# Nine blocks of each layer's down projection as seven block products instead of eight, with sums on VectorE

## What is computed

```
D_MODEL, SEQ, DEPTH, D_FF = 2048, 256, 2, 5632
def conv_ffn(x, w_gate, w_up, conv_w, conv_b, w_down):
    g, u = x @ w_gate, x @ w_up
    gc = conv_b + causal 3-tap convolution of g
    return (silu(gc) * u) @ w_down        # (256 x 5632) @ (5632 x 2048)
for l in range(DEPTH):
    x = layer_norm(ALPHA * x + mixer(x), ln1_g[l], ln1_b[l])
    x = layer_norm(ALPHA * x + conv_ffn(x, ...), ln2_g[l], ln2_b[l])
```

## Time and profile before

| what | value |
|---|---|
| median of 3 runs | 2224.84 us (2224.28 to 2224.9) |
| span of the profiled execution (its own time isn't given beside it) | 2222.5 us |
| PE busy | 2208.0 us, 99% |
| DVE, ACT, POOL busy | 1397.8, 1037.8, 244.1 us |
| first down stage, from the start of the span | 868.3 to 1107.8 us |
| second down stage | 1973.8 to 2213.5 us |

### The profile page before, as it was taken

One profiled execution on the slowest core, in us unless ns is written; L12 is line 12 of the kernel. 1 busy time (PEld: TensorE's weight loads), 2 busy tenths in 40 slices (PEclk: granted clock), 3 DMA queues, 4 the chain that ended last, 5 costly groups with the idle time before them and its releaser, 6 DMA issues.

```text
span 2222.5 us, 28282 instructions
## 1 busy us (share of the span) xinstructions
PE 2208.0 (99%) x11424; PEld 1892.6 (85%) x11424; DVE 1397.8 (63%) x1758; ACT 1037.8 (47%) x1295; POOL 244.1 (11%) x250
## 2 busy tenths in 40 slices
PE   9999999999999999999999999999999999999998
PEld 7888888888888888888888888888888888888886
DVE  6655576776667666544485566677766666664545
ACT  5444555444444444433454445554444444443343
POOL 1751000220000000000008410002200000000000
PEclk9999999999999999999999999999999999999999
DMA  8655565666666666666665555756666666666664
GB/s 278 194 167 160 157 215 174 189 190 190 190 190 189 190 189 205 219 192 193 190 190 170 162 162 150 225 173 189 189 190 189 190 189 190 189 211 215 191 195 155
DMA packets 214818, 420.92 MB, mean 189 GB/s; under 512 B 13056, under 2 KB 15136, under 8 KB 213664
## 3 DMA queue, kind: packets, MB, share of 16 engines
q1 hardware_dynamic: 211824, 406.37, 59.8%
q0 software_dynamic: 2432, 12.22, 1.6%
q10 hardware_dynamic: 432, 0.52, 0.1%
HBM read 416.97 MB, written 2.10 MB: 189 GB/s over the span
## 4 chain that ended last, share of the span: by engine, by line
PE 98%; DVE 1%; DMA 0%; ACT 0%; issue 0%; POOLq 0%; POOL 0%; SPq 0%; DVEq 0%
PE ps L1289 29%; PE ps L1177 16%; PE ps L1175 16%; PE ps L1176 16%; PE ps L1293 15%; PE ps L1220 1%; PE ps L1416 1%; PE ps L1390 1%; PE ps L1367 1%; DMA raw<-in_w_in_dram 0%; PE ps L1423 0%; PE ps L1163 0%; PE ps L1436 0%; PE ps L1437 0%; PE ps L1435 0%; PE ps L1454 0%
## 5 line engine op out<-in xcount | busy, mean ns | idle before, releaser
L820 DVE TENSOR_TENSOR wlo<-raw,whi 128x1024 fp32r<-128x1024 f32 x767 | 964.7, 1264 | 700.6 <-ACT whi L578 697.0
L578 ACT ACTIVATE whi<-raw 128x1024 fp32r<-128x1024 f32 x767 | 807.9, 1059 | 853.0 <-DMA raw<-in_w_down_dram 278.5
L1289 PE MATMUL ps<-xT,whi 128*128 128x512 f32 x2816 | 657.3, 390 | 0.0
L1289 PEld LDWEIGHTS ps<-xT,whi 128*128 128x128 f32 x2816 | 522.6, 188 | 104.3 <-ACT qkT L599 0.4
L1175 PE MATMUL ps<-whi,xT 128*128 128x512 f32 x920 | 369.0, 401 | 0.0
L1177 PE MATMUL ps<-whi,xT 128*128 128x512 f32 x920 | 359.3, 391 | 0.0
L1176 PE MATMUL ps<-wlo,xT 128*128 128x512 f32 x920 | 358.5, 390 | 0.0
L1293 PEld LDWEIGHTS ps<-xT,wlo 128*128 128x128 f32 x2816 | 350.6, 192 | 7.5
L1293 PE MATMUL ps<-xT,wlo 128*128 128x256 f32 x2816 | 352.9, 283 | 0.0
L1175 PE MATMUL ps<-whi,hT 128*128 128x512 f32 x696 | 270.9, 389 | 0.0
L1177 PE MATMUL ps<-whi,hT 128*128 128x512 f32 x696 | 270.9, 389 | 0.0
(11 more groups left out here) (203 smaller groups left out, 1203.5 us busy)
## 6 DMA issues: line engine op xcount, KB each, us to landing
raw<-in_w_gate_dram SPq DMA_DIRECT2D x176, 512.0 KB, 4.0
raw<-in_w_up_dram SPq DMA_DIRECT2D x176, 512.0 KB, 4.0
raw<-in_w_down_dram SPq DMA_DIRECT2D x176, 512.0 KB, 4.1
raw<-in_w_in_dram SPq DMA_DIRECT2D x175, 512.0 KB, 3.7
raw<-in_w_out_dram SPq DMA_DIRECT2D x64, 512.0 KB, 4.2
xres<-in_x_dram POOLq DMA_DIRECT2D x4, 512.0 KB, 5.7
lnb<-in_ln_g_dram POOLq DMA_DIRECT2D x2, 1024.0 KB, 7.5
lnb<-in_ln_b_dram POOLq DMA_DIRECT2D x2, 1024.0 KB, 10.4
```

Of the source, the lines that this page charges most:

```text
L578: act.activation(whi[:, s, :, :], raw[:, s, :, :], ACT.Copy).then_inc(hi_done, 1)
L820: dve.tensor_tensor(wlo[:, s, :, :], raw[:, s, :, :], whi[:, s, :, :].bitcast(F32), ALU.subtract)\
L1289: return pe.matmul(ps[:, bank, :], whi[:, s, kk, m * P:(m + 1) * P], xT[:, kt, :, :].rearrange("p a s -> p (a s)"), start=kt == 0, stop=kt ...
```

## The change

Take a pair of hidden tiles and two neighbouring chunks of columns (a half). The eight block products (2 token tiles x 2 hidden tiles x 2 chunks) become seven products of sums of blocks, by Strassen's method in Winograd's form. This is done for 5 pairs in half 0 (chunks 0, 1) and 4 pairs in half 1 (chunks 2, 3): nine **sets** a layer, numbered 0 to 8. Each takes the place of two groups; 70 groups stay, and group numbers below are the new ones. PE does set k right behind group `SET_AFTER[k]`.

```diff
+SETS_AT = ((11, 16, 20, 24, 28), (36, 41, 46, 51))
+SETS = [(half, i) for half in range(2) for i in range(len(SETS_AT[half]))]
+SET_AFTER = [SETS_AT[half][i] for half, i in SETS]
+SET_LOAD = [-1] + SET_AFTER[:-1]
+HALF_GROUPS = [2 * (GD - len(a)) for a in SETS_AT]
+PRODUCTS = ("A12", "S4", "A11", "S1", "S3", "S2", "A22")
+FACTORS = ("B21", "B22", "B11", "T1", "T3", "T2", "T4")
+TARGET = (0, 2, 4, 5, 7, 6, 1)
+SUMS = (((4,), (4, 6, 5)), ((4, 6, 7), (4, 6, 7, 5)))
...
+        sraw = nc.alloc_sbuf_tensor_at("sraw", [P, 7, CW], F32, offset=xT_at)
+        slo = nc.alloc_sbuf_tensor_at("slo", [P, 7, CW], F32R, offset=xT_at)
+        shi = nc.alloc_sbuf_tensor_at("shi", [P, 7, CW], F32R, offset=xT_at + 7 * CW * 4)
...
 SP
+                for n in range(DOWN):
+                    c, _, pair = down_group(n)
+                    load(w_down, layer, 0, BASE_DOWN + n, pair * GK, c * CW)
+                    if n - RING in SET_LOAD:
+                        k = SET_LOAD.index(n - RING)
...
+                        if layer + k > 0:
+                            sp.wait_ge(set_used, set_count(layer, k - 1))
+                        for kk in (1, 0):
...
+                            sp.dma_start(sraw[:, 2 * kk:2 * kk + 2, :].rearrange("p s n -> p (s n)"),
+                                         w_down[layer, row:row + P, half * 2 * CW:(half + 1) * 2 * CW])\
+                                .then_inc(set_in, 16)
...
 POOL
+                pool.wait_ge(set_used, set_count(layer, len(SETS) - 1))
                 carry_wait(pool, 3)
                 pool.dma_start(lnb2[:, 0, :], row(ln2_g, layer).broadcast_to([P, D_MODEL])).then_inc(ln2_in, 16)
-                wait_groups(pool, layer, BASE_DOWN + GD // 2)
                 pool.dma_start(lnb2[:, 1, :], row(ln2_b, layer).broadcast_to([P, D_MODEL])).then_inc(ln2_in, 16)
...
 ACT, behind split_hi of group n
+                for k, a in enumerate(SET_LOAD):
+                    if k < PREPARED and n == max(a + 6, 8):
+                        form_high(layer, k)
+                    part = n - max(a + 6, 8)
+                    if 0 <= part < 3:
+                        set_high(layer, k, part)
...
 DVE, behind split_lo of group n
+                for k, a in enumerate(SET_LOAD):
+                    at = max(a + 6, 8)
+                    if k < PREPARED and n == at - 1:
+                        form_sums(layer, k)
+                    if k < PREPARED and n == at + 1:
+                        form_low(layer, k)
+                    if n == at:
+                        set_sum(layer, k)
+                    if 0 < n - at < 4:
+                        set_low(layer, k, n - at - 1)
+                for half in range(2):
+                    summed = SETS_AT[half][-2] + 9
+                    if n == summed:
+                        y_chunk(layer, 1, 2 * half, in_banks(2 * half))
+                    if n == summed + 1:
+                        products(layer, 2 * half)
+                    if n == summed + 2:
+                        products(layer, 2 * half + 1)
+                if n == DOWN_ENDS[1] + LAG:
+                    y_chunk(layer, 1, 1, in_banks(1))
...
 PE
+            def set_of_products(layer, k):
...
+                for i, (name, factor) in enumerate(zip(PRODUCTS, FACTORS)):
+                    bank, first, last = TARGET[i], pair == 0, pair == len(SETS_AT[half]) - 1
+                    if first and bank == 2:
+                        wait_free(pe, layer, 2, ("down", 2 * half + 1))
+                    if first and bank >= 4:
+                        wait_free(pe, layer, bank, ("prod", half))
+                    pe.wait_ge(set_lo, 7 * (set_count(layer, k) - 1) + i + 1)
...
+                    pe.matmul(ps[:, bank, :], hi, shi[:, s, :], start=fresh, stop=False)
+                    pe.matmul(ps[:, bank, :], hi, slo[:, s, :], start=False, stop=False)
+                    ins = pe.matmul(ps[:, bank, :], lo, shi[:, s, :], start=False, stop=last and bank != 2)
+                ins.then_inc(set_used, 1)
```

More of the change, by code:

```diff
@@ L180 @@
 USES = bank_uses()
-FULL = [[u for u in bank if u[0] not in ("proj", "out", "down", "half")] for bank in USES]
+FULL = [[u for u in bank if u[0] not in ("proj", "out", "down", "half", "prod")] for bank in USES]
 PAR_LN = (2 * KT, 0)
@@ L196 @@
 POOL_PIECE = NC_OUT - 1
-GB_AT = (NC_OUT - 1) * GD + 6
+GB_AT = 62
 GAIN_BANKS, BIAS_BANKS = (4, 5, 6), (7, 0, 1)
@@ L881, in y_chunk, with products @@
                 link(last)
+            def products(layer, c):
+                cols = slice(c * CW, (c + 1) * CW)
+                if c % 2 == 0:
+                    for t in range(TT):
+                        wait_read(dve, layer, in_banks(c)[t], ("down", c))
+                for i in range(4):
+                    for t in range(TT):
+                        banks = SUMS[t][c % 2]
+                        if i >= len(banks):
+                            continue
+                        if i == 0 and c % 2 == 1:
+                            ins = dve.scalar_tensor_tensor(xres[:, t, cols], xres[:, t, cols], ALPHA,
+                                                           ps[:, banks[i], :], ALU.mult, ALU.add)
+                        else:
+                            ins = dve.tensor_tensor(xres[:, t, cols], xres[:, t, cols], ps[:, banks[i], :], ALU.add)
+                        link(ins)
+                if c % 2 == 1:
+                    for b in (4, 5, 6, 7):
+                        dve.nop().then_inc(psum_free[b], 1)
+                else:
+                    for t in range(TT):
+                        last = dve.bn_stats(stats[:, t, c, :], xres[:, t, cols])
+                    link(last)
@@ new lines, in set_low @@
+            def set_low(layer, k, part):
+                for i in ((0, 1), (2, 3, 4), (5, 6))[part]:
+                    name = FACTORS[i]
+                    if i == 0:
+                        dve.wait_ge(set_sums, 4 * set_count(layer, k))
+                    dve.wait_ge(set_hi, 7 * (set_count(layer, k) - 1) + i + 1)
+                    dve.tensor_tensor(slo[:, SLOT[name], :], sraw[:, SLOT[name], :],
+                                      shi[:, SLOT[name], :].bitcast(F32), ALU.subtract).then_inc(set_lo, 1)
@@ L1184, in rows_times_chunk @@
                         wait_free(pe, layer, banks[1], ("proj", 0))
-                    ins = rows_times_group(layer, n, stationary, kts, banks[t], t, first, last,
+                    ins = rows_times_group(layer, n, stationary, kts, banks[t], t, first and banks[t] != held, last,
                                            second_tile if t == 0 else None)
```

147 lines of the change are left out of this document (124 added, 23 removed).

## The result

| kernel | median | runs |
|---|---|---|
| before | 2224.84 us | 2224.28 to 2225.7 (5) |
| after | 2232.37 us | 2231.74 to 2233.07 (5) |

The ratio is 1.0034, 95% interval 1.0021 to 1.0046: **slower by 7.5 us, 0.34%**. The forecast was 2227.1, no change within 0.2%, with a range of 2219.5 to 2238. The time lies in the range, but the change is over 0.2%: it is the "slower" case, which had 0.38.

What follows compares the result with a forecast made beforehand. PE's queue of matmuls was taken to bound the down projection. 14.6 us of waits and restarts added, 12.2 of matmuls removed: +2.3 us on the median 2224.84 gives 2227.1, range 2219.5 to 2238.

Steps and rivals of the forecast that it cites:

- "slower" case: Rival: a set's load takes as long as a queued one, 6.3 us, giving 2237 us; chance 0.38.
- Matmuls removed: Down projection on PE: 54 matmuls less at 0.2268 us each, 12.2 us less.
- Chain of a set: Load, DVE list and last products take 16.96 us against 15.65 available; PE waits 1.3 us at sets 2, 3, 4.
- The set's load: 1 MB on SP's queue, issued when PE finishes the previous set (T0), lands at T0 + 5.15 us.
- Change of halves: From set 4 to set 5: PE waits 1.55 us for split 36, 1.35 for bank 2, 2.9 a layer.
- Restart: Weight loads exposed after PE waits, 0 to 0.19 us on some five waits a layer; 0.9 us in all.
- Granted clock: PE's clock in the down stages: under 1.00 was listed as a sign the prediction is wrong, with no cost in the sum.
- The floor of the range: Set's load lands like 512 KB, T0 + 3.85; 0.6 us a set stays, halves keep 1.6; 2219.4 us.
- Layer norm loads behind set 8: Two 1 MB loads issued together, about 7.2 us of delay; cost nothing, bound 0 to 2 us a layer.
- the ring: Weight slots loaded ahead of PE in the down projection; claimed to have 7.5 us to spare.
- The load's two prices from the Trainium skill: For a set's 1 MB load: formula 4.4 us, table 6.15 us; neither used, table's case chance 0.1.
- VectorE's overlap: DVE operations that wait for nothing start 0.60 us apart; rival without overlap: 0.7 us a set, 2233, chance 0.03.

Runs made afterwards that it cites:

- e5: e4 with set 0's low parts back behind splits 9, 10, 11 and its high parts spread likewise; 2212.43 us, 0.9945 of the kernel before.
- e6: Changed kernel with the hidden state's low parts placed before the set's sums on DVE; 2228.69 us, 1.0018 of the kernel before.
- e3: Changed kernel with only the sets' positions moved, at least five groups apart; 2225.86 us, 1.0006 of the kernel before.
- e7: Changed kernel with each set's load behind the next group's load in SP's queue; 2305.77 us, 1.0365 of the kernel before.
- e1: Changed kernel without the eleven adds of `products` in the first half, so the output lacks these sums; 2224.2 us, 0.9999 of the kernel before.
- e8: Kernel before with chained unused DVE operations behind split 30, 14 in layer 0 and 17 in layer 1; 2231.34 us, 1.0032.
- e2: Changed kernel with each set's high and low parts together behind its sums, hidden state's low parts before them; 2238.19 us, 1.0057 of the kernel before.
- e4: e2 with `products` adds spread over five groups, set 5's steps at group 38, second half's sets later; 2219.78 us, 0.9980 of the kernel before.

## Why the prediction came out as it did

**Matmuls removed, 12.2 us:** right. The count is 54, and e5, where nothing waits, gains 12.0.

**Chain of a set, 16.96 us, 1.3 us of wait at the third and sixth product of sets 2, 3, 4:** the mechanism is right, the place too, and DVE's list took 10.43 us instead of 10.45. Sets 0, 1 and 5 to 8 don't wait. e6 and e3 confirm that it is this chain. But it came out at 17.4 to 18.2 us, 12.0 us of excess at the six sets where 7.8 were forecast, and the term that was too small is the load.

**The set's load, T0 + 5.15:** the term that was mis-sized most. It landed at T0 + 5.37 to 6.22 where it counts (sets 2 to 5 of both layers), T0 + 5.64 in the mean, with T0 as the start of the set's last matmul plus 0.23. The prediction's own price was 0.8 us for each 0.1 us, which gives an estimate of 3.9 us for these 0.49. So **the slower rival** was right in part: it named this chain with nothing spare on it, and T0 + 5.45 as the point from which the result is slower by over 0.2%. Its size, 6.3 us for a load that is queued, was not reached by any load that PE waited for in this kernel. e7, where the load really stands behind another, shows the same chain at 4.8 us later: 73 us.

**Change of halves, 1.55 at group 36 and 1.35 at bank 2:** place right, sizes off. Group 36 started 2.6 and 2.4 us late (2.43 and 2.26 by the list): set 5's load landed 5.5 and 5.3 us after its issue, not 5.0, and and DVE stood still for 0.43 us before split 36, where the four `nop`s that free banks stand, a step I had at nothing. The bank 2 wait didn't appear in either layer, since the halved clock delayed PE past it; in layer 0 of e6, without the halved clock, it does, with 1.0 us.

**Restart, 0.9 us in all:** right in sum, though not as I had it. The restart is 0.11 us on each of 15 waits, but in a set the wait at the sixth product absorbs that of the third, so about eight of them count, 0.9 us.

**Granted clock:** missing from the sum. I named a clock under 1.00 only as a sign of error. It cost 3.2 us, and e1 shows that it hangs on the wait at group 36 alone. It took the place of the bank 2 waits, forecast at 2.7, so the sum lost little by it. That is luck: two errors of opposite sign.

Together: 14.6 forecast; 3.9 more for late loads, 0.9 for the stop at the `nop`s, 3.2 for the clock, 2.7 less for bank 2, makes 19.9; measured were 20.5. The rest is in part the 0.05 us between DVE's end and PE's start at each wait (957.33 to 957.38 above), some 0.4 over eight such chains. (The floor of the range, 2219.4, was added up without the 0.9 of restart; that changes nothing here.)

**Layer norm loads behind set 8:** right, nothing, and split 58 was ready 14.6 us after set 8 (forecast 14.4, wanted at 16.35). The delay was 8.3 us where 7.2 were forecast, more than the 7.5 I gave the ring to spare; it did no harm since DVE's own list was the later of the two.

**The load's two prices from the Trainium skill** ("DMA: Bandwidth & Descriptors", sections "Anatomy of one DMA" and "Bandwidth"): in sets 1 to 8 the set's load landed 5.2 to 6.0 us after its issue, between the estimate of 4.4 by the formula and the table's 6.15. **VectorE's overlap**: two low parts in 1.28 us again, so the 0.60 of the earlier trace rows held. The section of the Trainium skill that the prediction set against it ("VectorE: DVE Perf Modes", "The DRAIN you can't avoid") itself adds that a next operation that is not held starts earlier, and with that the trace agrees: operations of 0.68 us start 0.60 apart.

## What to carry to other kernels

Work taken off a saturated engine shows only if the engines that feed it don't come late, and in-order lists make that a matter of position, not of load: DVE had time enough on average, and the same operations in another order, with the second half's sets two groups later, turn +7.5 us into -12.0. Write down the chain from one use of a single buffer to the next (load, each operation of the feeding engine in program order, the part of the use that must follow) and compare it with the time between uses; then look at the same list where the rarer work falls in, at the start and between the halves. Here a wait of PE cost its listed length plus about 0.3 us, and one of over 2 us mostly, but not always, another 1.4 to 2.7 us. And price the load by its range: half a microsecond on a chain that is run through eight times was the largest error here.

## What the runs showed of the hardware

- A wait of PE costs 0.27 us beyond its listed length, in the distance of the first matmul and the one behind it (0.77 and 0.11 for a listed 0.61): 0.16 since the list counts from the modelled end of the matmul before, 0.11 of restart.
- After waits of 2.26, 2.36, 2.43, 2.76, 2.77, 3.01, 3.5, 3.79 and 4.0 us the matmuls come 0.43 apart, the lower clock level, for 5 to 12 of them; after 1.0, 1.5 and 1.8 us (e8, e2) they don't, nor after 2.20 us in e6 (layer 0) and 2.56 us in e4 (layer 1). In e7, with waits at each set, they do after 1.80 us and don't after 2.25. What decides between 1.8 and 2.6 us these runs don't tell.
- With SP's queue empty, a set's load of 1 MB in two DMAs landed 5.2 to 6.0 us after its issue (sets 1 to 8, 16 loads, 5.5 in the mean); one DMA of 512 KB takes 3.7.
- `nop`s that only free PSUM banks are probably not free: DVE stood still for 0.43 us where four of them follow the last add, in both layers, and again in e5, where they stand at another place, and for 0.04 us at most behind adds without them. No run leaves them out, so that they are the cause is not shown.
- Two layer norm loads of 1 MB issued together held back the ring's weights by 8.3 us, where one alone cost 3.6.
